# A hybrid decoder step whose experts are visited in the order of their row counts, with three matmul widths

## The reference

```python
acc = sum over experts e of
    combine[:, e] * ((silu(x @ w_gate[e]) * (x @ w_up[e])) @ w_down[e])   # 1024 -> 512 -> 1024
y = RMSNorm(x + acc)
```

## Time and profile before

| | us |
|---|---|
| median of 3 runs | 877.75 |
| lowest and highest run | 877.45, 877.9 |
| profiled execution, span | 877.9 |
| PE busy | 845.3 |
| DVE, ACT, POOL busy | 526.8, 383.5, 244.6 |
| the experts' part, first gate matmul to the end | 431.9 to 877.9 |

### The profile page before, as it was taken

One profiled execution on the slowest core, in us unless ns is written; L12 is line 12 of the kernel. 1 busy time (PEld: TensorE's weight loads), 2 busy tenths in 40 slices (PEclk: granted clock), 3 DMA queues, 4 the chain that ended last, 5 costly groups with the idle time before them and its releaser, 6 DMA issues.

```text
span 877.9 us, 15841 instructions
## 1 busy us (share of the span) xinstructions
PE 845.3 (96%) x5828; PEld 749.4 (85%) x5828; DVE 526.8 (60%) x1237; ACT 383.5 (44%) x734; POOL 244.6 (28%) x272
## 2 busy tenths in 40 slices
PE   6999999999999999998899999999999999999993
PEld 5989879999988787775789988889988999888992
DVE  5537424657778435557585676656666656766573
ACT  7545303656367425544334434344343444433442
POOL 1000000000000110002045654447545555445472
PEclk9999999999999999999599999999999999999997
DMA  9121001102222182336188889978899887898871
GB/s 291 43 97 47 2 0 49 49 1 56 49 96 96 59 274 91 150 145 216 60 275 290 300 304 325 306 271 310 291 310 324 307 288 278 290 360 295 286 256 50
DMA packets 118505, 166.56 MB, mean 190 GB/s; under 512 B 17012, under 2 KB 95928, under 8 KB 118469
## 3 DMA queue, kind: packets, MB, share of 16 engines
q1 hardware_dynamic: 103109, 135.48, 45.7%
q0 software_dynamic: 15360, 30.59, 10.2%
HBM read 146.84 MB, written 41.17 MB: 214 GB/s over the span
## 4 chain that ended last, share of the span: by engine, by line
PE 47%; another core or an unknown queue 1%; ACT 1%; issue 1%; DVE 0%; POOL 0%; ACTq 0%; POOLq 0%
PE bank L1912 31%; PE bank L1922 4%; PE bank L1933 3%; PE bank L1924 3%; PE bank L1923 3%; PE bank L1900 2%; PE bank L1893 1%; ACT split L2012 1%; POOL out L1820 0%; PE bank L1905 0%; DVE wdlo L2116 0%; PE bank L1939 0%; DVE x L2188 0%; ACT hs L2014 0%
## 5 line engine op out<-in xcount | busy, mean ns | idle before, releaser
L1912 PE MATMUL bank<-big,ring 128*128 128x160 f32 x2048 | 286.1, 301 | 0.1
L1912 PEld LDWEIGHTS bank<-big,ring 128*128 128x128 f32 x2048 | 281.9, 191 | 1.4
L1836 POOL TENSOR_TENSOR hold_at<-ident 128x1 f32<-128x1 f32 x63 | 53.1, 842 | 175.3 <-DVE lists L2083 128.4
L2116 DVE TENSOR_TENSOR wdlo<-wdn,split 128x1024 fp32r<-128x1024 f32 x64 | 76.7, 1219 | 0.0
L2008 ACT ACTIVATE sg<-bank 128x160 f32<-128x160 f32 x64 | 19.5, 304 | 109.7 <-PE bank L1912 95.4
L2012 ACT CAST split<-wdn 128x1024 fp32r<-128x1024 f32 x64 | 64.9, 1039 | 0.0
L502 PE MATMUL bank<-split,ring_r 128*128 128x384 f32 (+1 forms) x192 | 64.4, 336 | 0.1
L504 PE MATMUL bank<-split,ring_r 128*128 128x384 f32 (+1 forms) x192 | 61.7, 321 | 0.0
L2111 DVE TENSOR_TENSOR hs<-hid,hs 128x128 fp32r<-128x128 f32 x64 | 18.9, 295 | 57.3 <-ACT hs L2014 46.8
L1922 PE MATMUL bank<-split,hs 128*128 128x512 f32 x128 | 52.6, 411 | 0.0
L1399 PE MATMUL bank<-split,ring_r 128*128 128x512 f32 (+1 forms) x128 | 51.7, 404 | 0.3 <-PEq L1191 0.3
(11 more groups left out here) (390 smaller groups left out, 1788.4 us busy)
## 6 DMA issues: line engine op xcount, KB each, us to landing
wdn<-in_w_down SPq DMA_DIRECT2D x32, 1024.0 KB
ring<-in_w_gate SPq DMA_DIRECT2D x32, 1024.0 KB, 5.4
ring<-in_w_up SPq DMA_DIRECT2D x32, 1024.0 KB
ring<-in_w_in SPq DMA_DIRECT2D x8, 1024.0 KB, 5.9
x<-in_x_prompt SPq DMA_DIRECT2D x8, 512.0 KB, 6.1
h_rows<-h SPq DMA_DIRECT2D x8, 512.0 KB, 2.6
sums<-x SPq DMA_DIRECT2D x8, 512.0 KB, 3.6
v<-in_x_prompt SPq DMA_DIRECT2D x4, 512.0 KB, 5.4
```

What stands on the lines that cost most here:

```text
L1836: nc.gpsimd.tensor_tensor(hold_at[:], ident[:, 0:1], ident[:, 1:2], ALU.add).then_inc(e_hold, 1)
L1912: x = nc.tensor.matmul(bank[f % 2][:, side * 256:side * 256 + W], ring[:, u, k, c0:c0 + P], xT[:, k, :], start=k == 0, stop=k == KC - 1)
L2116: nc.vector.tensor_tensor(wdlo[:, k, :], wdn[:, k // 2, (k % 2) * D:(k % 2 + 1) * D], wdhi[:, k, :].bitcast(F32), ALU.subtract).then_inc(e ...
```

## The change

Experts 1 to 15 are visited in the order of their row counts, smallest first (expert 0 stays first). DVE sorts them on the chip at the start of `b3_all` (`order_experts`) and writes the order to `ids`; SP and DVE load the expert's number from there in each step (`expert`). Steps 1 to 6 do gate and up with 132 columns, steps 7 to 12 with 144, steps 13 to 15 and step 0 with 160. A row whose rank lies beyond its expert's width is moved to a second round; where an expert has more rows than its width, the number of rounds is raised. All gate parts now come ahead of all up parts, each part with a PSUM bank of its own, and the product is taken right from the bank of up. Gate and up weights are loaded with input rows 8p + k on partition p, so that a run is 8 KB; the normed rows are stored to HBM in the matching order. The loads of `n` and `m` move behind the first step.

```diff
+WIDTHS = [(1, 132), (7, 144), (13, W)]
@@ b2_all
-        nc.gpsimd.memset(later[:, :, 0:1], 0.0).then_inc(r_fl, 1)
...
-        nc.gpsimd.tensor_copy(table[:, :, :, 5].rearrange("p (g j) t -> p t g j", g=NG),
-                              later[:].unsqueeze(2).broadcast_to([P, TT, NG, 4])).then_inc(r_fl, 1)
...
-                nc.vector.scalar_tensor_tensor(out=h2[0:r, j % 2, :], in0=x1[0:r, j, :], scalar=rstd[0:r, j:j + 1],
+                nc.vector.scalar_tensor_tensor(out=turned(h2[0:r, j % 2, :]), in0=by_lane(x1[0:r, j, :]),
...
-        link(nc.vector.tensor_reduce(mxc[:, 0:1], bank[6][:, 0:NE], axis=AX.X, op=ALU.max))
...
+        nc.vector.tensor_copy(order.counts, bank[6][:, 0:NE])
@@ expert_unit
-        w = (A["w_gate"], A["w_up"])[u % 2].rearrange("l e (k p) n -> (l e) p k n", p=P)
-        return ring[:, u, :, :], w[e, :, :, (u // 2) * 256:(u // 2 + 1) * 256]
+        w = (A["w_gate"], A["w_up"])[u // 2].rearrange("l e (p h k) n -> (l e) p h k n", p=P, h=2)
+        return ring[:, u, :, :].rearrange("p (k a) n -> p k (a n)", k=4), w[e, :, u % 2, :, :]
@@ b3_all, sync
-            e = (i + 1) % NE
+            e = expert(sp, (i + 1) % NE)
...
-                    sp.wait_ge(e_gu, i * 4 + (2 if u < 2 else 4))
+                    sp.wait_ge(e_gu, i * 8 + (4 if u < 2 else 8))
@@ b3_all, tensor
+        def gate_or_up(i, side, f, w):
             for k in range(KC):
+                if f == 0 and k % 4 == 0:
+                    pe.wait_ge(e_w[2 * side + k // 4], i * 16 + 16)
+                x = nc.tensor.matmul(bank[f][:, 0:w], mats[:, side, k, f * P:(f + 1) * P], xT[:, k, 0:w],
                                      start=k == 0, stop=k == KC - 1)
+            x.then_inc(e_gu, 1)
...
-        def step(i, first, last):
+        def step(i, first, last, w):
             pe.wait_ge(e_xe, i * 3 + 3)
             for f in range(4):
+                if f >= 1 and not first:
+                    pe.wait_ge(e_z, i * 3 + f // 3)
+                gate_or_up(i, 0, f, w)
...
+            for f in range(4):
+                pe.wait_ge(e_si, i * 4 + f + 1)
+                gate_or_up(i, 1, f, w)
...
-        with pe.Fori(1, n - 1) as i:
-            step(i, False, False)
+        for j, (a, w) in enumerate(WIDTHS):
+            with pe.Fori(a, WIDTHS[j + 1][0] if j + 1 < len(WIDTHS) else n - 1) as i:
+                step(i, False, False, w)
@@ b3_all, scalar, one step: four silus, then
+            weights_hi(0)
+            weights_hi(1)
+            gated_hi(0)
+            weights_hi(2)
+            gated_hi(1)
+            weights_hi(3)
+            gated_hi(2)
+            gated_hi(3)
@@ b3_all, vector
+        def order_experts():
+            link(nc.vector.scalar_tensor_tensor(out=key[:], in0=counts, scalar=float(NE), in1=numbers, op0=ALU.mult,
+                                                op1=ALU.add))
...
+            nc.vector.tensor_copy(ids[:], part[0:1, :]).then_inc(e_order, 1)
...
+            link(nc.vector.tensor_copy(table[:, 1:, :, 5].rearrange("p e t -> p t e"), seen[:, :, 1:]))
...
+            if first:
+                next_lists(first_lists())
+                third_table()
...
+            weights_lo(i, 0)
+            gated(0)
+            weights_lo(i, 1)
+            gated_lo(i, 0)
+            gated(1)
+            weights_lo(i, 2)
+            gated_lo(i, 1)
+            gated(2)
+            weights_lo(i, 3)
+            gated_lo(i, 2)
+            gated(3)
+            gated_lo(i, 3)
```

More of the change, by code:

```diff
@@ L73, in __init__ @@
         self.s1, self.s2, self.gp, self.w1 = take(TT), take(TT), take(TT), take(TT)
+class Order:
+    def __init__(self, big):
+        self.counts = big[:, 3712:3712 + NE]
+        self.both = big[:, 3728:3728 + 4 * TT].rearrange("p (t j) -> p t j", t=TT)
 class Samples:
@@ L188, in program @@
         lists0 = sb("lists0", [P, 2], I32)
+        order = Order(big)
         s_w = [sem(f"s_w{j}") for j in range(5)]
@@ L1195, in b2_all @@
 def b2_all(nc, A, O, S0, Sp, s_w, samples, halves, sb, sem, e_w, wdn, bank, ident, onesf, eps_c, uT, gT, ring, x1, x_rows, h2_dram,
-           sums_dram, rank_m, table, iota_w, steps, once, weighing, rows_0):
+           sums_dram, rank_m, table, iota_w, order, weighing, rows_0):
     c2 = ExitStack()
@@ L1216, in b2_all @@
     wr = picks.rearrange("p a t e -> p (a t e)")[:, 0:KC * SB].rearrange("p (k c) -> p k c", k=KC)
-    later = sb("later", [P, TT, 4], ctx=c2)
-    both = sb("both", [P, TT, 4], ctx=c2)
+    both = order.both
     Mb = sb("Mb", [P, TT, NE], BF16, ctx=c2)
@@ L1715, in b3_all @@
 def b3_all(nc, A, O, S0, samples, sb, sem, e_w, ring, wdn, bank, ident, eps_c, rows, h2_dram, sums_dram, rank_m, table, iota_w, steps,
-           once, weighing, rows_0):
+           once, order, rows_0):
     c3 = ExitStack()
@@ L1756, in b3_all @@
     e_hold = sem("e_hold")
+    e_sort, e_order, e_steps = sem("e_sort"), sem("e_order"), sem("e_steps")
+    compared = sb("compared", [P, NE, NE], ctx=c3)
+    within = sb("within", [P, NE, 4], ctx=c3)
+    earlier = sb("earlier", [P, TT, NE, 4], ctx=c3)
+    most = sb("most", [P, 2], ctx=c3)
+    limits = sb("limits", [P, ROUNDS], ctx=c3)
+    key, place, shift, part = [sb(x, [P, NE], ctx=c3) for x in ("key", "place", "shift", "part")]
+    ids = sb("ids", [1, NE], I32, ctx=c3)
     e_rk = sem("e_rk")
@@ L1769, in b3_all, with expert @@
     blk = block.enter_context(nc.Block())
+    def expert(eng, i):
+        return eng.value_load(ids[0:1, bass.ds(i, 1)], min_val=0, max_val=NE - 1)
     def count(eng):
+        eng.wait_ge(e_steps, 1)
         return eng.value_load(steps[0:1, 0:1], min_val=NE, max_val=NE * ROUNDS)
@@ L1849, in _ @@
         rows_old()
+        n = count(pool)
         with pool.Fori(0, n - 1) as i:
@@ L1956, in step @@
                     indices(facts)
-                if f == 0 and not first:
+                if f == 1 and not first:
                     pe.wait_ge(e_sql, i)
                     left_sums()
+            for f in range(4):
+                pe.wait_ge(e_si, i * 4 + f + 1)
+                gate_or_up(i, 1, f, w)
             if not last:
@@ L2037, in step @@
                 left_root()
-        with act.Fori(0, n - 1) as i:
+        step(0, False)
+        n = count(act)
+        m = last_step(act)
+        with act.Fori(1, n - 1) as i:
             step(i, False)
@@ L2144, in step, with gated @@
             if first:
-                first_lists()
-            for f in range(4):
-                dve.wait_ge(e_si, i * 4 + f + 1)
-                nc.vector.tensor_tensor(hid[:, f, :], sg[:, f % 2, :], bank[f % 2][:, 256:256 + W],
-                                        ALU.mult).then_inc(e_h, 1)
-                if first and f == 0:
-                    next_lists()
-                if first and f == 1:
-                    third_table()
-                if last and f == 1:
-                    nc.vector.tensor_tensor(S0[:], S0[:], samples.added, ALU.add).then_inc(e_state, 1)
-                gated_lo(i, f)
-                for k in ((0,), (1,), (2, 3), ())[f]:
-                    weights_lo(i, k)
+                next_lists(first_lists())
+                third_table()
+            if last:
+                nc.vector.tensor_tensor(S0[:], S0[:], samples.added, ALU.add).then_inc(e_state, 1)
+            def gated(f):
+                dve.wait_ge(e_gu, i * 8 + f + 5)
+                nc.vector.tensor_tensor(hid[:, f, :], sg[:, f, :], bank[f][:, 0:W], ALU.mult).then_inc(e_h, 1)
+            if not last:
+                e = expert(dve, (i + 3) % NE)
+            weights_lo(i, 0)
[10 more added lines that the diff above has]
+            gated_lo(i, 3)
             if not last:
@@ L2231, in _ @@
         step(0, True, False)
+        n = count(dve)
+        m = last_step(dve)
         with dve.Fori(1, n - 1) as i:
```

149 lines of the change are left out of this document (87 added, 62 removed).

## The result

The changed kernel takes 907.8 us (904.6 to 914.1 in four runs) against 877.8 us for the kernel before: 1.034 times the time, 95% interval 1.031 to 1.037. It is slower, and outside the range of the prediction. The profiled execution has a span of 908.1 us.

What follows compares the result with a forecast made beforehand. PE bounds the kernel now (96% busy), with a circle of DVE, POOL and DMA just behind that becomes the bound; 877.9 - 19.5 (steps and late silus) + 3.5 (start) = 861.9, say 862 us; range 846 to 882.

Steps and rivals of the forecast that it cites:

- Columns: PE's gate and up matmuls: 114 and 124 ns at 132 and 144 columns, steps 3.0 or 1.7 us shorter.
- Sort and register loads: Start of the kernel: DVE's sort delays step 0's end, PE's register loads move behind it; +3.5 us in all.
- The circle becomes the bound: Loop of DVE, POOL and DMA from lists_now to lists_now, without PE, bounds steps 1 to 12; chance 0.56.
- The circle takes 25.5 us: Round from lists_now to lists_now: 26.4 us less 0.9 us, against PE's 26.84 us step; bounds 24.7 or less to 27.9.
- the wait for the sums: POOL's wait in each round for its stored sums, 2.1 us in the mean, to get 0.9 us shorter.
- both as nothing: Result stores slowed beside DVE's subtractions (2.01 instead of 0.98 us), set against the gate load's earlier end: counted 0.
- longer weight runs delay POOL's stores: Rival: in POOL's stores, sums and results land a microsecond later each; circle 27.5 us, 888 us, slower; chance 0.17.
- two such hits: Two of DVE's four subtractions L2116 hitting POOL in full would put the circle at 27.5 us.

Runs made afterwards that it cites:

- the changed kernel without the wait: Changed kernel with result stores reading copied lists, lists_now no longer waiting for landed results, POOL waiting a round later: 854.2 us; with 1 KB runs 853.2 us.
- both kernels here: Changed kernel with w_up and w_down, or all loads of a step, issued only once the results have landed: 881.8 us and 910.3 us.

## Why the prediction was wrong

The sign was wrong: 862 us was forecast, and 907.8 us lies outside the range.

- **Columns**: right. 113.4 and 123.5 ns; steps of 23.73, 25.02 and 26.72 us, once they were free, against 23.6, 24.9 and 26.6.
- **Sort and register loads**: right within half a microsecond, +4.0 against +3.5.
- **The circle becomes the bound**: right. PE idle ahead of the second gate part, DVE waiting in most rounds.
- **The circle takes 25.5 us**: this step failed. The forecast took a mean round of 26.4 us, named two waits in it that can move, and priced one: the wait for the sums, 0.9 us less. Most of that came: 2.4 to 1.7 us. The other wait, for the landing of the results, 3.6 us of the same round, was left as it was without a reason. It became 5.9 us. The four stores were set against an earlier end of the gate load, "both as nothing", and became 0.6 us longer. In the first round DVE's wait ahead of `lists_next` came on top, 3.85 us, which is gone with an eighth of the weight bytes. A round is 28.8 us instead of some 25.7 (twelve of 25.5, three of about 26.6), and 15 x 3.1 = 46 us is the whole error.
- **Why the landing grew**: the forecast made PE faster and kept the release of the loads in place. PE releases them. Shown is that the loads make the landing long (1.2 us with none beside it, 1.4 us with an eighth of their bytes), and that narrow columns bring the loss with either order of products. In the changed kernel none of the thirteen rounds is left in which the loads were issued far enough ahead of the results; such rounds landed in 2.1 us before. Had all thirteen been like the other seven, at 4.9 us, 1.3 of the 2.3 us would be explained. The rest is open, and so is what fixes the issue times; PE now waits for the sums in most rounds and so releases the loads at a set time behind them, which would do it, but no run isolates this.
- **The rival "longer weight runs delay POOL's stores"** had the place and the sign (888 us, slower, from 26.8 us on), and its "for" was so: in twelve of the thirteen rounds w_up is issued within some 2 us of the last store's end. Its cause, the length of the run, is refuted. It was given 0.17, with a price of one microsecond for each landing; the results took 2.3 us more and the sums 0.7 us less. The Trainium skill (DMA: Bandwidth & Descriptors, "Queues, rings and completion order"), which it leaned on, says that an engine drains a whole packet from one ring before the next. No run here shows a turn; what they show is that 45765 and 103109 packets for the same bytes delay the results alike, by 5.9 and 5.4 us.

The version to keep is the changed kernel without the wait, at 853 to 854 us: 2.7% below before.

## What to carry to other kernels

Before an engine is made faster, price each wait of the circle that will bound next, its landings one by one; and ask which transfers the faster engine will release sooner and whose landing they will meet. Where a step's weights must share the DMA engines with a chain of small stores, moving the loads can just move the wait, as it did in both kernels here: take the landing off the chain with a second buffer, here a copy of 32 bytes a partition.

## What the runs showed that was not expected

More columns made the kernel faster (896 against 908 us), and loads delayed on purpose gained 26 us.

Even with hardly any weights the four result stores took longer, 6.1 us against 5.3. The timelines of POOL and DVE of that kernel:

```profile
524.64 2.05 POOL L1833 DMA_INDIRECT out<-x,lists_now  x1 [0.16 <-issue]
...
524.58 1.22 DVE L2195 TENSOR_TENSOR wdlo<-wdn,split 128x1024 fp32r<-128x1024 f32 x1
```

A store that starts as a subtraction of `wdlo` does takes 2.05 us here; elsewhere such a store takes about 1.0 us. The Trainium skill (SBUF — State Buffer, "Who interferes with whom"), which the prediction cited, has a DVE instruction with two SBUF inputs contend with a GpSimd instruction that reads SBUF. The trace agrees in kind. The prediction reckoned with 2 us a round for two such hits; the four stores got some 0.8 us longer in the mean.

The granted clock of PE was 0.89, as a mean, over the step of 30.58 us above, in which PE paused for 3.9 us, and 1.00 over the one of 24.24 us. PE is not on the chain there, so this cost nothing; with the pauses gone the granted clock is 1.00 in the three steps shown of the kernel without the wait.
